# Splitting a normed sum tile by tile: 128 tokens at a time, each tile transposed into two PSUM banks of its own

## The reference

```python
def rms_norm(x, gain):
    xf = x.astype(jnp.float32)
    y = xf * lax.rsqrt(jnp.mean(xf * xf, axis=-1, keepdims=True) + RMS_EPS)
    return (y * gain.astype(jnp.float32)).astype(x.dtype)
...
        h = h + mix.astype(h.dtype)
        h = h + swiglu(rms_norm(h, ffn_norm[i]), ffn_w_gate_up[i], ffn_w_down[i]).astype(h.dtype)
```

## Time and profile before

| what | value |
|---|---|
| median of 3 runs | 1881.06 us (1879.68 to 1881.2) |
| profiled execution, whole | 1878.88 us |
| profiled execution, span | 1877.3 us |
| TensorE busy | 1693.8 us, 90% |
| VectorE busy | 1139.8 us, 61% |
| ScalarE busy | 863.8 us, 46% |
| GpSimd busy | 243.8 us, 13% |
| mean granted TensorE clock | 0.955 |

### The profile page before, as it was taken

One profiled execution on the slowest core, in us unless ns is written; L12 is line 12 of the kernel. 1 busy time (PEld: TensorE's weight loads), 2 busy tenths in 40 slices (PEclk: granted clock), 3 DMA queues, 4 the chain that ended last, 5 costly groups with the idle time before them and its releaser, 6 DMA issues. The chain is left out here.

```text
span 1877.3 us, 25093 instructions
## 1 busy us (share of the span) xinstructions
PE 1693.8 (90%) x10106; PEld 1472.9 (78%) x10106; DVE 1139.8 (61%) x1464; ACT 863.8 (46%) x1059; POOL 243.8 (13%) x205
## 2 busy tenths in 40 slices
PE   4999999989999987589999999988979899989988
PEld 3777888879987865479988678767879878779976
DVE  3887666755554454645546775347887565567754
ACT  5344556644433553244444423364544554345542
POOL 1653240000000000000000610004444100000000
PEclk9999999989999998799999999988989899989999
DMA  5552445645555343146645404100000155445533
GB/s 201 173 177 98 135 133 181 202 128 180 185 167 195 127 157 122 58 157 183 191 155 168 137 1 138 45 17 1 1 1 1 46 181 179 157 146 179 178 126 123
DMA packets 161906, 240.97 MB, mean 128 GB/s; under 512 B 12640, under 2 KB 80992, under 8 KB 161664
## 3 DMA queue, kind: packets, MB, share of 16 engines
q1 hardware_dynamic: 154400, 232.81, 38.1%
q10 hardware_dynamic: 7104, 4.64, 0.9%
q0 software_dynamic: 288, 1.92, 0.3%
HBM read 238.29 MB, written 1.05 MB: 127 GB/s over the span
## 5 line engine op out<-in xcount | busy, mean ns | idle before, releaser
L197 DVE TENSOR_TENSOR wlo<-raw,whi 128x2048 fp32r<-128x2048 f32 x224 | 524.3, 2352 | 309.3 <-ACT whi L191 298.8
L191 ACT ACTIVATE whi<-raw 128x2048 fp32r<-128x2048 f32 x224 | 420.4, 1887 | 302.3 <-PE ps L328 258.1
L326 PE MATMUL ps<-xs,whi 128*128 128x256 f32 (+1 forms) x1312 | 387.4, 295 | 18.3 <-DVE xs L460 7.7
L327 PE MATMUL ps<-xs,whi 128*128 128x256 f32 (+1 forms) x1312 | 386.0, 294 | 0.0
L328 PE MATMUL ps<-xs,wlo 128*128 128x256 f32 (+1 forms) x1312 | 385.8, 294 | 0.0
L326 PE MATMUL ps<-whi,xs 128*128 128x512 f32 x672 | 275.8, 410 | 19.0 <-DVE wlo L197 11.2
L326 PEld LDWEIGHTS ps<-xs,whi 128*128 128x128 f32 x1312 | 250.1, 191 | 27.2 <-issue 20.7
L327 PE MATMUL ps<-wlo,xs 128*128 128x512 f32 x672 | 270.7, 403 | 0.0
L328 PE MATMUL ps<-whi,xs 128*128 128x512 f32 x672 | 270.1, 402 | 0.0
L327 PEld LDWEIGHTS ps<-xs,whi 128*128 128x128 f32 x1312 | 250.2, 191 | 5.7
L328 PEld LDWEIGHTS ps<-xs,wlo 128*128 128x128 f32 x1312 | 250.0, 191 | 5.8
(11 more groups left out here) (366 smaller groups left out, 2394.3 us busy)
## 6 DMA issues: line engine op xcount, KB each, us to landing
raw<-in_ffn_w_gate_up SPq DMA_DIRECT2D x88, 512.0 KB, 4.7
raw<-in_a_w_in SPq DMA_DIRECT2D x72, 512.0 KB, 4.6
raw<-in_w_in SPq DMA_DIRECT2D x60, 512.0 KB, 4.6
raw<-in_w_mod SPq DMA_DIRECT2D x48, 512.0 KB, 4.6
raw<-in_w_up SPq DMA_DIRECT2D x44, 512.0 KB, 4.7
raw<-in_ffn_w_down SPq DMA_DIRECT2D x40, 512.0 KB, 4.5
raw<-in_b_w_in SPq DMA_DIRECT2D x24, 512.0 KB, 4.6
raw<-in_w_down SPq DMA_DIRECT2D x20, 512.0 KB, 4.1
```

Of the source, the lines that this page charges most:

```text
L191: self.hi_ok.inc(act.activation(self.whi[:, h % NHI, 0:nk, :], self.raw[:, h % NRAW, 0:nk, :], ACT.Copy))
L197: self.lo_ok.inc(dve.tensor_tensor(self.wlo[:, h % NRAW, 0:nk, :], self.raw[:, h % NRAW, 0:nk, :], self.whi[:, h % NHI, 0:nk, :].bitcast(F ...
L326: pe.matmul(o, ahi, bhi, start=start, stop=False)
L327: pe.matmul(o, ahi, blo, start=False, stop=False)
```

## The change

`Norm.split` no longer uses the class `Split` (which stays, for the other splits). Tile `t` is transposed into the banks `bank + 2t` and `bank + 2t + 1`, four blocks in each, and each filled bank is signalled. ScalarE and VectorE then go through the four banks in the order tile 0 low blocks, tile 0 high blocks, tile 1 low blocks, tile 1 high blocks. Without a shift each bank is four pieces of 128x128 on ScalarE and four on VectorE. With a shift VectorE modulates four pieces of 128x128 a bank, and the copy and the subtraction stay one instruction a bank (128x4x128 into `xs`). Tile 0's high parts are signalled by `as_`, tile 1's by `xs_hi`.

```diff
-            parts = Split(lambda t, k: self.xn[:, t, k * P:(k + 1) * P], 0, self.stage, self.scale, self.shift, self.perm, self.bank)
+            xs_want[:] = [xs_hi.n + 2, xs_hi.n + 4]
+            tr0, mod0, half0 = xs_tr.n, xs_mod.n, as_.n
             if ahead is not None:
                 ahead(0)
                 pe.wait_ge(added.sem, added.n)
             for t in range(TT):
                 pe.wait_ge(st_ready.sem, self.ready[t])
-                parts.tile_on_pe(t)
-            W.hi(last)
-            parts.on_act()
+                for k in range(KT):
+                    i_ = pe.transpose(self.seen(t, k), self.xn[:, t, k * P:(k + 1) * P], ident)
+                    if k % 4 == 3:
+                        xs_tr.inc(i_)
             if ahead is not None:
                 ahead(1)
+            W.hi(last)
+            if ahead is not None:
                 W.lo(last)
-                parts.on_dve()
-            else:
-                parts.on_dve()
+            his = []
+            for t in range(TT):
+                for g in range(2):
+                    if self.shift is not None:
+                        dve.wait_ge(xs_tr.sem, tr0 + 2 * t + g + 1)
+                        for k in range(4 * g, 4 * g + 4):
+                            i_ = dve.tensor_scalar(self.staged(t, k), self.seen(t, k), self.scale[:, k:k + 1], self.shift[:, k:k + 1],
+                                                   ALU.mult, ALU.add)
+                        xs_mod.inc(i_)
+                        act.wait_ge(xs_mod.sem, mod0 + 2 * t + g + 1)
+                        his.append(self.high_part(t, g, act.activation(self.part(0, t, g), self.staged4(t, g), ACT.Copy)))
+                    else:
+                        act.wait_ge(xs_tr.sem, tr0 + 2 * t + g + 1)
+                        for k in range(4 * g, 4 * g + 4):
+                            i_ = act.activation(xs[:, 0, k, t * P:(t + 1) * P], self.seen(t, k), ACT.Copy, scale=self.scale[:, k:k + 1])
+                            if t and k == 4 * g + 1:
+                                xs_hi.inc(i_)
+                        his.append(self.high_part(t, g, i_))
+            for t in range(TT):
+                for g in range(2):
+                    dve.wait_ge(*his[2 * t + g])
+                    if self.shift is not None:
+                        i_ = dve.tensor_tensor(self.part(1, t, g), self.staged4(t, g), self.part(0, t, g).bitcast(F32), ALU.subtract)
+                    else:
+                        for k in range(4 * g, 4 * g + 4):
+                            i_ = dve.scalar_tensor_tensor(xs[:, 1, k, t * P:(t + 1) * P], self.seen(t, k), self.scale[:, k:k + 1],
+                                                          xs[:, 0, k, t * P:(t + 1) * P].bitcast(F32), ALU.mult, ALU.subtract)
...
+        def seen(self, t, k):
+            return ps[:, self.bank + 2 * t + k // 4, (k % 4) * P:(k % 4 + 1) * P]
```

More of the change, by code:

```diff
@@ new lines, in split @@
+            for t in range(TT):
[7 more added lines that the diff above has]
+                                                          xs[:, 0, k, t * P:(t + 1) * P].bitcast(F32), ALU.mult, ALU.subtract)
+                            if t and k == 4 * g + 1:
+                                xs_lo.inc(i_)
+                    if t:
+                        xs_lo.inc(i_)
@@ new lines, in split, with high_part, staged @@
+            if self.shift is not None:
+                xs_want[:] = [xs_hi.n - 1, xs_hi.n]
+            if ahead is None:
+                W.lo(last)
+        def high_part(self, t, g, i_):
+            sig = xs_hi if t else as_
+            sig.inc(i_)
+            return sig.sem, sig.n
+        def seen(self, t, k):
+            return ps[:, self.bank + 2 * t + k // 4, (k % 4) * P:(k % 4 + 1) * P]
+        def staged(self, t, k):
+            return self.stage[:, 2 * t + k // 4, (k % 4) * P:(k % 4 + 1) * P]
@@ L570, in add_product, with staged4, part @@
+        def staged4(self, t, g):
+            return self.stage[:, 2 * t + g, :].rearrange("p (k n) -> p k n", k=4)
+        def part(self, q, t, g):
+            return xs[:, q, 4 * g:4 * g + 4, t * P:(t + 1) * P]
     def add_product(chunks, nxt, norm, gate=None, tmp=None):
```

## The result

| what | before | changed |
|---|---|---|
| median of 20 runs each | 1879.83 us (1876.15 to 1881.90) | 1883.17 us (1879.37 to 1886.19) |
| ratio | | 1.0016, interval 1.0009 to 1.0023 |
| profiled execution, whole | 1878.88 us | 1883.87 us |
| profiled execution, span | 1877.3 us | 1882.1 us |
| mean granted TensorE clock | 0.955 | 0.953 |

The changed kernel is slower by 3.0 us (1.7 to 4.3). The forecast was 5.9 us and the time 1887.0, range 1883.5 to 1891.0. The sign is right, the size is not: the time lies 0.3 us under the range, and 3.0 us is within the 0.2% that the prediction called no change. The miss of 3.8 us has two parts: the median of before, 1881.06 us over 3 runs and 1879.83 over 20, makes 1.2 of it, and the change itself, which cost 3.3 us between these medians and not 5.9, the other 2.6.

What follows compares the result with a forecast made beforehand. TensorE was taken to wait at five splits for VectorE's last piece, behind ScalarE's queue where there is no shift. Terms 3.9 + 1.1 + 0.9 = +5.9 us on the median 1881.06 gave 1887.0 us, range 1883.5 to 1891.0.

Steps and rivals of the forecast that it cites:

- What bounds the kernel: At the splits without a shift TensorE waits on ScalarE's queue, its first pieces, then all VectorE pieces; with one, VectorE alone.
- The price of a piece: In the splits, halving a piece saves a third: steps 0.25 us on ScalarE, 0.26 on VectorE, 0.32 for a modulation.
- The stops: TensorE's idle time ahead of its products after each split: 5.1 to 5.2 us without a shift, 1.6 and 6.6 with.
- places 1 and 3: Into the first and second feed-forward layers, without a shift: TensorE's start later by 1.3 us each.
- 4 and 5: Into the hybrid layer and the last feed-forward layer, with a shift: TensorE's start later by 1.1 and 0.9 us.
- all of it in front of TensorE: At the three splits without a shift, VectorE's later end delays TensorE in full: +1.3 us each, 3.9 together.
- everything behind that start moves with it: TensorE waits for a split's last piece, so all later work shifts equally; without a shift +1.3 us each.
- place 2: Into the second block, without a shift: TensorE's start later by 1.3 us.
- The clock rival: Behind the stops: the clock falls once more or slow stretches grow; 1889 us, up to 1891; chance 0.20.
- Its main case: Stop into the hybrid layer, grown to 1.6 us, makes the clock fall, costing 1.9 us; chance 0.20 with growing slow stretches.
- The rival of a later cover: Behind a split, a weight load or GpSimd table was TensorE's next wait and covers part; 1882 to 1885 us; chance 0.07.
- The rival of tile 0's pieces: At the splits, tile 0's pieces finish before tile 1 is normed: 3 to 6 us less, 1875 to 1878; chance 0.03.

Runs made afterwards that it cites:

- two instructions more: Kernel before with two more VectorE instructions ahead of the split's last signal in the four places other than the hybrid layer's; one execution, 1882.35 us.
- the halves: Kernel before, but TensorE starts the three feed-forward layers when the half of xs its first products read is there; 0.9958 (-7.9 us), again 0.9961 (-7.3 us).
- the two halves of the change: Two kernels against the one before: new split only in the three places without a shift, 1.0023 (+4.3 us); only in the two with one, 1.0014 (+2.6 us).
- the weight half out of the way: New split in the three places without a shift, ScalarE's W.hi(last) moved behind it, against the kernel before: 1.0004 (0.9992 to 1.0015).
- +0.39, +0.77, +1.17 and +2.3 us: Kernel before with one, two, three or six more VectorE instructions in four stops: 1882.14 us, 1882.35 us (one execution each), 1.0025, 1.0064.
- a trace with the same instructions as before up to 1027 us: Kernel before with the new split only in the two places with a shift, hybrid and last feed-forward layer: 1.0014, +2.6 us.
- three kernels: Against the kernel before: new split only without a shift, 1.0023; W.hi(last) moved behind the split without a shift, new split there 1.0004, old split 1.0012.

## Why the prediction was wrong

**What bounds the kernel: right.** The chain of ScalarE's queue, its first pieces, VectorE and TensorE ends last in the trace after as before.

**The price of a piece: right.** From start to start ScalarE took (4.22 - 0.409) / 15 = 0.254 (taken 0.257 or 0.25) and VectorE (4.23 - 0.343) / 15 = 0.259 (taken 0.26). The modulation, for which no row stood, took (5.19 - 0.410) / 15 = 0.319, where 0.32 was taken between the bounds 0.26 and 0.453, from the nearest size of the same operation less what 128 elements are worth. By the formula of the Trainium skill's page "VectorE: DVE Perf Modes", section on the TRN2 errata, 128 elements from PSUM come to an estimated 0.26 us. The scalar_tensor_tensor agrees with it (0.259), the modulation with two columns doesn't (0.319). The +4 us that this estimate gives for the whole would have been nearer to the median, but by a term that the trace contradicts.

**The stops: right.** 5.16 us at places 1 and 3, 1.63 and 6.57 us at 4 and 5, each within 0.03 us of the forecast.

**The step that failed: "all of it in front of TensorE", so that "everything behind that start moves with it".** The sum took a stop's growth as time lost, one for one. In the traces that was so at place 4 alone. At places 1, 3 and 5 it cost 0.59, 0.71 and 0.51 us instead of 1.3, 1.3 and 0.9, and at place 2 1.88 instead of 1.3. Together 4.80 instead of 5.9. The row was there: the earlier trace rows shows the restart of place 1 at a granted clock of 0.50, and the prediction used it only to say that the clock had nothing left to lose. It should have asked where the slow part ends, and whether that end moves with the restart. The end doesn't, up to a point, and so a later restart saves slow time. Nor does everything behind the start move with it for good: with two instructions more, 2.2 us of lag were gone again ahead of place 3.

**The clock rival: the right place, one sign only.** It let the slow parts grow by "a few tenths each". They shrank by 1.5, 1.3 and 0.8 us at three places and grew by 1.2 at one. Its main case, a fall of the clock at the stop of place 4, did not come: the clock there is 1.00 with a stop of 1.6 us.

**From 4.8 to 3.0.** The span of the profiled execution grew by 4.8 us, near enough to the places. In that lag are +1.5 us at 104 to 110, which comes and goes between executions of one kernel (the halves show it once and once not), and -1.4 us of slow parts elsewhere, of which the -1.66 near 1080 to 1100 came in both traces of the changed kernel and in neither of before. Without the first the lag would be 3.4 us, between the measured 3.0 and 3.9. That sum fits, and the fall at 104 to 110 isn't the change's, since seven of fourteen traces have it on the same work. But a sum over two single traces doesn't show what the medians of many executions are made of. Of the 2.6 us by which the change cost less than forecast, the places account for 1.1; the other 1.5, and why the two halves of the change cost 6.9 us together, stay open.

**The range.** Its low end, 1883.5, was +2.4 us above the median of before that it was made against, 1881.06, and took in the lowest price of a modulation, 0.26 us, and a part of a delay taken up later. The measured +3.0 is inside that. The time is outside because the median of before over 3 runs lay 1.2 us above that over 20; the prediction took it as exact, though the profiled execution beside it was 2.2 us lower. The working of the sum had nothing for the clock on the low side, which is what was needed. With half of each growth counted where the restart is at a low clock, the sum would have been (3 x 1.3 + 0.9) / 2 + 1.1 = +3.5 us; that it is so near to the medians would be luck in part, since place 2 cost 1.88 and not 0.65. The rival of a later cover named the right times, 1882 to 1885, with a chance of 0.07, but by a wait that isn't there. The chance of 0.80 for slower by over 0.2% was too high for the same reason: a step of +4.8 at the places, or the +3.0 of the median, is too near to 3.8.

**The rival of tile 0's pieces** was set aside for the right reason, and was right on what it needs: with the weight half out of the way the stop is 3.36 us.

## What to carry to other kernels

Where an engine restarts at a low granted clock, a stop isn't worth its length: find the end of the slow part in the windows behind the restart, and count half of what is added or saved as long as that end stays, and more than all of it where the end moves. Take such an estimate with both signs, since the same 1.3 us cost 0.6 at one place and 1.9 at another, and take more than one trace, since where a slow part lies can differ between executions of the same instructions. And look at what a wait asks for before cutting the work into finer pieces: finer pieces behind a full queue only add their fixed price, while letting the first product wait for the half that it reads made the kernel 7 to 8 us faster.

## What was unexpected in the hardware

- The cost of a stop is a staircase: +0.39, +0.77, +1.17 and +2.3 us at place 2 cost 0.12, 1.81, 1.88 and 2.62 us.
- Second traces of before and of the changed kernel agree to 0.06 us at all five places, those of the kernel with halves differ by 0.6 and 1.2 us at two, and a trace with the same instructions as before up to 1027 us cost 0.61 us more at place 1. Place 5, untouched, cost 0.8 us more in three kernels.
- At place 3 the clock fell 7.60 to 7.83 us behind the same matmul in all fourteen traces, though this matmul starts up to 9.3 us earlier or later in the program. Lag that was there before it had been given back in part.
- Work ahead of any edit differs by 1.5 us between traces (104 to 110, granted clock 1.00 or 0.83). One trace's total can't be trusted to a few us. The way between fixed matmuls is better, good to some 0.6 us at one place.
